# One conditioning tile behind each weight split in the down stages, and the residual scaling inside the up stage

## The reference, cut to what matters

```python
x = x + (jax.nn.silu(h_gate) * h_val) @ w_ffn_down[l]      # block 1, first down stage
return rms_norm(x, final_norm_g)
...
c_act = jax.nn.silu(c)
ada = c_act @ w_ada[l] + b_ada[l]                          # 1024 -> 9216
(sh1, sc1, g1, sh2, sc2, g2, sh3, sc3, g3) = jnp.split(ada, 3 * ADA_SUBLAYERS, axis=-1)
h = modulate(rmsnorm(x, ffn1_norm[l]), sh1, sc1)
x = x + FFN_RES_WEIGHT * g1[:, None, :] * swiglu(h, ffn1_w_in[l], ffn1_w_out[l])
h = modulate(rmsnorm(x, mix_norm[l]), sh2, sc2)
z = h @ w_in[l]
```

## Time and profile before

| | |
|---|---|
| time, median of 3 runs | 973.43 us (973.12 to 976.32) |
| time of the profiled execution | 973.2 us |
| its span, first to last instruction | 971.5 us |
| mean granted PE clock, as a share of full speed | 0.991 |
| busy: PE / DVE / ACT / POOL | 936.1 / 705.0 / 466.1 / 87.2 us |
| read from memory | 189.89 MB, 197 GB/s over the span |
| first down stage (halves 0 to 21) | from 292.67 us; additions from 355.50 |
| second down stage | from 497.94 us; additions from 566.79 |

### The profile page before, as it was taken

One profiled execution on the slowest core, in us unless ns is written; L12 is line 12 of the kernel. 1 busy time (PEld: TensorE's weight loads), 2 busy tenths in 40 slices (PEclk: granted clock), 3 DMA queues, 4 the chain that ended last, 5 costly groups with the idle time before them and its releaser, 6 DMA issues.

```text
span 971.5 us, 19979 instructions
## 1 busy us (share of the span) xinstructions
PE 936.1 (96%) x7412; PEld 902.9 (93%) x7412; DVE 705.0 (73%) x1086; ACT 466.1 (48%) x702; POOL 87.2 (9%) x122
## 2 busy tenths in 40 slices
PE   7999999999999999999998989999999999999996
PEld 5989998999999988999998979899999899999996
DVE  6499766888889967878789877666667666655544
ACT  4654665655553435443342445655554643334432
POOL 2043301000001210100002141000000000000000
PEclk9999999999999999999998999999999999999999
DMA  7333326555657983988879945443355265556641
GB/s 241 131 131 109 109 93 233 173 184 186 187 177 278 410 350 100 340 277 274 267 256 349 409 149 174 155 149 109 118 166 183 80 215 173 179 189 189 199 151 44
DMA packets 53324, 191.57 MB, mean 197 GB/s; under 512 B 5920, under 2 KB 6432, under 8 KB 53152
## 3 DMA queue, kind: packets, MB, share of 16 engines
q1 hardware_dynamic: 41760, 149.96, 46.6%
q0 software_dynamic: 10656, 39.33, 11.2%
q10 hardware_dynamic: 864, 1.67, 0.5%
HBM read 189.89 MB, written 1.05 MB: 197 GB/s over the span
## 4 chain that ended last, share of the span: by engine, by line
PE 83%; DVE 9%; DMA 4%; ACT 2%; issue 2%; DVEq 0%; ACTq 0%; SPq 0%; POOLq 0%
PE ps L331 24%; PE ps L333 23%; PE ps L332 23%; DMA raw<-w 3%; DVE w_lo L1077 2%; PE ps L419 2%; PE ps L469 2%; PE ps L405 1%; PE ps L394 1%; DVE rstd L1082 1%; PE ps L395 1%; PE ps L396 1%; DVE ada_raw L1339 1%; ACT w_hi L749 1%; DMA cols<-cols_in 1%
## 5 line engine op out<-in xcount | busy, mean ns | idle before, releaser
L331 PE MATMUL ps<-xh,w_hi 128*128 128x256 f32 x1472 | 422.2, 287 | 11.3 <-DVE xl L1103 9.9
L333 PE MATMUL ps<-xh,w_lo 128*128 128x256 f32 x1472 | 417.6, 284 | 0.0
L332 PE MATMUL ps<-xl,w_hi 128*128 128x256 f32 x1472 | 417.6, 284 | 0.0
L1077 DVE TENSOR_TENSOR w_lo<-raw,w_hi 128x1024 fp32r<-128x1024 f32 x282 | 342.2, 1233 | 99.3 <-ACT w_hi L749 99.0
L749 ACT ACTIVATE w_hi<-raw 128x1024 fp32r<-128x1024 f32 x282 | 288.4, 1054 | 132.4 <-PE ps L333 81.2
L331 PEld LDWEIGHTS ps<-xh,w_hi 128*128 128x128 f32 x1472 | 283.6, 193 | 17.4 <-issue 10.4
L332 PEld LDWEIGHTS ps<-xl,w_hi 128*128 128x128 f32 x1472 | 283.7, 193 | 0.3 <-issue 0.2
L333 PEld LDWEIGHTS ps<-xh,w_lo 128*128 128x128 f32 x1472 | 283.5, 193 | 0.0
L331 PE MATMUL ps<-act_hi,w_hi 128*128 (+1 forms) x528 | 150.5, 285 | 6.2 <-DVE w_lo L1077 6.2
L332 PE MATMUL ps<-act_lo,w_hi 128*128 (+1 forms) x528 | 149.0, 282 | 0.0
L333 PE MATMUL ps<-act_hi,w_lo 128*128 (+1 forms) x528 | 148.9, 282 | 0.0
(11 more groups left out here) (242 smaller groups left out, 994.6 us busy)
## 6 DMA issues: line engine op xcount, KB each, us to landing
raw<-w SPq DMA_DIRECT2D x282, 512.0 KB, 4.3
ada_raw<-ada_w POOLq DMA_DIRECT2D x72, 512.0 KB, 7.0
X<-x_in SPq DMA_DIRECT2D x4, 256.0 KB, 6.5
bm<-bias_in POOLq DMA_DIRECT2D x1, 1024.0 KB, 5.0
out<-X SPq DMA_DIRECT2D x4, 256.0 KB, 2.1
tab<-tab_in ACTq DMA_DIRECT2D x1, 640.0 KB, 9.4
gmask<-gmask_in ACTq DMA_DIRECT2D x1, 512.0 KB, 11.5
cact<-c_in POOLq DMA_DIRECT2D x1, 512.0 KB, 4.8
```

Of the source, the lines that this page charges most:

```text
L331: pe.matmul(o, lh, rh, start=start, stop=False, skip_group_check=True)
L332: pe.matmul(o, lh, rl, start=False, stop=False, skip_group_check=True)
L333: return pe.matmul(o, ll, rh, start=False, stop=stop, skip_group_check=True)
L1077: v.tensor_tensor(w_lo[:, slot(h), :], raw[:, slot(h), :], w_hi[:, slot(h), :].bitcast(F32), ALU.subtract).then_inc(lo_ready, 1)
```

## The change

Three things. In a down stage with conditioning tiles, the group of four ahead of the loop goes away: the tiles begin behind the first split, one behind each of the loop's 16 splits, and two behind each of the last four. The scaling leaves the second down stage; the up stage's loop is cut in three, (0,1), (1,3) and (3,5) in units of four steps, with the reciprocal and four scalings after the first piece and the other four after the second. The number of instructions of each kind stays. Only DVE's order changes.

```diff
-            def ffn_up(fi, c0, ada0=None):
+            def ffn_up(fi, c0, ada0=None, between=((0, None), (5, None))):
...
-                with dve.Fori(0, (FT - 2) // 4) as i:
-                    for vv in range(4):
-                        up_step(conv, fi, c0 + 2 + vv, 2 + vv, i=i * 2)
-                        if ada0 is not None:
-                            ada(ada0 + 4 + vv, i=i)
-
-            def ffn_down(n, c0, mod=None, gate=None, last=False, residual=None, ada0=None):
-                if residual:
-                    residual(0)
-                    residual(1)
+                for (i0, part), (i1, _) in zip(between, between[1:]):
+                    if part is not None:
+                        fin1_residual(part)
+                    with dve.Fori(i0, i1) as i:
+                        for vv in range(4):
+                            up_step(conv, fi, c0 + 2 + vv, 2 + vv, i=i * 2)
+                            if ada0 is not None:
+                                ada(ada0 + 4 + vv, i=i)
+
+            def ffn_down(n, c0, mod=None, gate=None, last=False, ada0=None):
                 if ada0 == 0:
                     dve.wait_ge(cact_ready, 1)
-                if ada0 is not None:
-                    for k in range(4):
-                        ada(ada0 + k)
                 with dve.Fori(0, 4) as i:
                     for vv in range(2):
                         for half in range(2):
                             lo(c0 + 2 + vv, i=i, halves=(half,))
                             if ada0 is not None:
-                                ada(ada0 + 4 + 2 * vv + half, i=i)
-                for half in range(2):
-                    lo(c0 + 10, halves=(half,))
+                                ada(ada0 + 2 * vv + half, i=i)
+                for k in range(2 if last else 4):
+                    lo(c0 + 10 + k // 2, halves=(k % 2,))
                     if ada0 is not None:
-                        ada(ada0 + 20 + half)
-                if not last:
-                    for half in range(2):
-                        lo(c0 + 11, halves=(half,))
-                        if ada0 is not None:
-                            ada(ada0 + 22 + half)
+                        ada(ada0 + 16 + 2 * k)
+                        ada(ada0 + 17 + 2 * k)
...
-            ffn_up(1, C_UP[1], ada0=24)
-            ffn_down(2, C_DN[1], mod=(1, 2, 0.5), gate=0, residual=fin1_residual, ada0=48)
+            ffn_up(1, C_UP[1], ada0=24, between=((0, None), (1, 0), (3, 1), (5, None)))
+            ffn_down(2, C_DN[1], mod=(1, 2, 0.5), gate=0, ada0=48)
```

## The result

| | before | changed |
|---|---|---|
| time, median | 975.2 us (973.12 to 977.79, 7 runs) | 980.26 us (979.27 to 984.54, 7 runs) |
| ratio to before | | 1.006, 95% interval 1.0042 to 1.0078 |
| profiled execution: time, span | 973.2, 971.5 us | 980.15, 978.5 us |
| mean granted PE clock | 0.991 | 0.984 |
| first down stage, to the next stage's first matmul | 78.23 us (292.67 to 370.90) | 84.30 us (293.48 to 377.78) |

The kernel is slower by 0.6%, outside the predicted range (971.0 to 979.0). The table by stage says where: the first down stage lost 6.1 us, the second gained nothing, and the up stage carries the scaling for nothing. Behind it (from 579.57 and from 586.46 on) both kernels need the same time to 0.1 us.

The account below looks back on a forecast made before the run. The prediction took TensorE (PE) to bound the kernel, with 83% of the chain of waits. First stage +2.0 + 1.95 and second -4.14 + 1.95 gave +1.8 us on 973.2, so 975.0 us, range 971.0 to 979.0.

Parts of the forecast that it names:

- The entries: Start of both down stages: PE starts half 4 without waiting for its split, -1.15 us first stage, -7.66 second.
- The scaling in the up stage: Up stage: the moved reciprocal and scalings cost nothing, cover enough by 0.5 us; bounds 0 and 1 us.
- rival (d): Up stage: the 0.5 us cover fails and PE waits on a split near 411 us; about 976; chance 0.06.
- The clock at the exits: End of both down stages: clock falls behind the idle time, 1.95 us each, +3.9 us; bounds 0 and 2 x 2.31.
- The tail: Last four splits of each down stage, two tiles each: DVE sets the pace, tile 20's reload adds 0.61 us.
- First norm matmul of the stage: PE's restart after each down stage's exit wait, entry included: +2.0 us in the first stage, -4.14 in the second.
- Rival (a): Tail of both down stages bound by the DMA: at landings of 8.3 us each exit 2.7 us later, 980.4; chance 0.27.

Follow-up runs that it names:

- e1: The kernel before with only the scaling moved into the up stage, the four tiles staying ahead of the down loops; 970.74 us, 0.9973 of before.
- e9: The changed kernel with 10 matmuls of a constant, which nobody reads, ahead of each exit wait; 976.49 us, 1.0027 of before.
- e8: The changed kernel with e5's pairs at the front and e6's tiles among the additions, none behind the last four splits; 970.92 us, 0.996 of before.
- e14: The kernel before with only POOL's setup work held back until behind the norm after the second down stage; 971.19 us, 0.9968 of before.
- e5: The changed kernel with two tiles behind each of the first four splits and one behind the others; 973.67 us, 0.9995 of before.
- e3: The changed kernel without the loads of tiles 20 to 23 in both down stages, products made from old buffer contents; 975.37 us, 1.0013 of before.
- e6: The changed kernel with each down stage's last four tiles moved among and behind the additions, one behind each of 20 splits; 965.77 us, 0.9899 of before.
- e13: e6 with POOL's setup work held back until behind the norm after the second down stage; 960.18 us, 0.9857 of before.

## Why the prediction was wrong

Predicted 975.0, measured 980.26 us. In the profiled executions it is +6.95 us where the sum had +1.8. Point by point:

- **The entries: right.** No wait at half 4 in either stage. -1.15 and -7.66 us were forecast; PE came to its exit wait 1.84 and 8.26 us earlier in its stage than before. The surplus of 0.6 each is a half's pace of 2.82 us where I had read 2.85.
- **The scaling in the up stage: right.** 127.01 for 127.04 us; rival (d) did not occur. e1 shows that the move by itself is a gain.
- **The clock at the exits: right in kind, a little small in the profiled execution.** I took 1.95 us an exit between bounds of 0 and 2.31. Behind the restart it cost 2.41 and 2.47 us, together 1.0 us of the miss; by the medians e9, with the clock kept, gave back 1.9 each, so over all runs the size was about right. That is in part luck. The 1.95 was a mean with 1.60 from the earlier trace rows, and those 1.60 us were not the clock's: with the clock at 1.00 the changed kernel needs the same 7.64 us there. The wait of 5.22 us and its 2.31 were the nearer case.
- **The tail: this step failed.** It read: "The three after it follow without a further wait." I costed the reload of tile 20 alone, with the least landing of the trace, and got 0.61 us. The first load did land as I had said (5.5 us for 5.6), and cost 0.48. But the pair frees a second buffer 1.14 us later, and its load took 7.4 us: 1.79 us of wait for tile 21, and 0.33 for tile 23. The waits were 2.60 and 2.53 us, 2.0 and 1.9 more than forecast; PE's faster pace, 2.82 us a half, took some 0.5 off again. I had written the warning into the same text, as a rate: three loads per group ask for 458 GB/s, and "at 409 a group would take 3.85 us, 1.6 us more per tail" than without waits. I then did not use it.
- **The sum of the miss.** First norm matmul of the stage, forecast +2.0 and -4.14, measured +3.66 and -2.43: 3.4 us. Low clock: 1.0 us. Start-up of this execution: 0.8 us. That makes the 5.2 us between +1.8 and +6.95. The last of these terms is chance, not mechanism, and the run medians moved too: the prediction stood on 973.43, and before measured 975.2 in the later set. By the ratio of the medians the change costs 0.6% where +0.16% was forecast.

Rival (a), the tail bound by the DMA, was the right mechanism with the right sign (980.4), and I gave it 0.27. Its form was not quite what happened: it had every landing at 8.3 us. In fact the median landing of the stage fell from 8.0 to 6.2 us. What hurt is the second load of a pair (7.4 us for tile 21, 7.8 for tile 23), and that its 980.4 lies so near the 980.26 is luck.

The Trainium skill (DMA: Bandwidth & Descriptors, Where 436 GB/s comes from) has about 358 GB/s as the limit of HBM reads for a core. The changed kernel does not follow it either: a window of 15 us shows 384 GB/s, and PE kept 2.82 us a half there.

```profile
330.00:345.00 15.00, 15.00 (x131) 15.00 (x130) 12.71 (x18) 5.88 (x6) 2.64 (x5) 1.00 0.99 384
```

What stays open: why a half follows the last after 2.82 us in some stages and after 2.85 in others (both of before and of e8, e1's and e14's first, e5's second). The stages with 2.85 don't share a DMA rate or a wait of PE that I could name. It is worth 0.6 us a stage. Why the second load of a pair is slow is open as well: that both share the DMA engines with the weights' loads is my reading of the trace, not shown. What was tried on the chip is only that without the loads the waits are gone (e3, but for 0.49 us on tile 19, whose load it keeps), and that without pairs they are gone too (e6).

## What to carry to other kernels

Filler work that reloads its own buffer has two prices, the engine's time and the buffer's way back (here 1.14 and about 7 us with four buffers); bunched at the head, the front or the tail of a stage it waits for the second, so spread it, and put the rest where its engine waits for the consumer anyway. Cost a stall of PE of several microseconds together with the half-speed stretch behind it (1.5 to 2.5 us here), but only where PE itself sets the pace behind the stall. When a small engine's setup work (POOL's memsets and sums) has slack, tie its start to the end of the critical work on the engine beside it, not to the first moment at which it may run.

## What the runs showed of the hardware

- DVE's TENSOR_SCALAR of 128x256 (L1126 in e6) takes 0.41 us with POOL quiet and took 3.28 where it met POOL's memsets: it ended at 569.68, the last memset at 569.53. In the changed kernel it started later and took 0.57, ending at 584.39 behind a memset that ended at 584.24. A TENSOR_TENSOR at 565.94 in e6 took its usual 0.42 us beside a memset, but one at 570.66 took 0.94 beside POOL's sums of two tensors. The Trainium skill (SBUF — State Buffer, SBUF: two separate sides) describes it: VectorE and GpSimd share a pair of ports under an exclusive lock, which a VectorE operation in a two-port mode needs against any GpSimd operation, and one with two SBUF inputs only against a GpSimd operation that reads SBUF. The rows agree, if TENSOR_SCALAR is taken to run in such a mode, which no run here shows. Moving POOL's work was worth 5.6 us (e13 against e6) and 3.3 us (e14 against before, of which the rows at the norm show 2.7) by the medians.
- A landing of 5.5 and then 7.4 us for two loads of 512 KB issued 1.14 us apart, beside the stream of weights.
- A stretch at half clock is free where PE waits for another engine anyway: 7.63 us with the clock down and 7.64 at 1.00 for the two halves behind the norm.
- Matmuls of 128x384 in float32 on a constant took 0.65 us each (20 in 13.1 us), and ten of them kept the clock at 1.00 up to a restart that came as late as in the changed kernel.
